# One transformer block with product-key experts on one core: split blocks inside the attention heads, scatter in pieces, four late value buffers, two row dots per ranked head

## The reference, cut to what matters

```python
mod = silu(c) @ w_ada + b_ada                         # six rows of 1024
h = rmsnorm(x) * (1 + scale1) + shift1
qa, ka, va, qb, kb, vb, ga, gb = split(h @ w_in)      # 512,128,128,512,512,512,1024,1024
ya = swa_sink_attention(rope(qa), rope(ka), va) @ w_up_swa    # 8 heads, 2 kv heads, window 128
yb = stick_breaking_attention(qb, kb, vb) @ w_up_sb           # 8 heads, causal
x = x + gate1 * ((sigmoid(ga) * ya + sigmoid(gb) * yb) @ w_out)
h2 = rmsnorm(x) * (1 + scale2) + shift2
# PEER: per head two lists of 128 key scores, the best 16 of each, the best 16 of their sums
# -> 8 x 16 experts of 128 x 128 for each token, softmax gate g
act = gelu(h2 . expert_u[e]) * g[e];   x = x + gate2 * sum_e act[e] * expert_v[e]
out = rmsnorm(x)
```

## Time and profile before

| | us |
|---|---|
| median of 3 runs (1956.57 to 1959.97) | 1956.68 |
| the profiled execution, device time | 1958.36 |
| its span, first to last instruction | 1956.4 |
| TensorE busy | 1815.1 |
| VectorE busy | 1325.8 |
| ScalarE busy | 693.5 |
| GpSimd busy | 535.2 |
| mean granted clock of TensorE | 0.949 |

### The profile page before, as it was taken

One profiled execution on the slowest core, in us unless ns is written; L12 is line 12 of the kernel. 1 busy time (PEld: TensorE's weight loads), 2 busy tenths in 40 slices (PEclk: granted clock), 3 DMA queues, 4 the chain that ended last, 5 costly groups with the idle time before them and its releaser, 6 DMA issues.

```text
span 1956.4 us, 24506 instructions
## 1 busy us (share of the span) xinstructions
PE 1815.1 (93%) x8747; PEld 1500.4 (77%) x8747; DVE 1325.8 (68%) x2755; ACT 693.5 (35%) x1072; POOL 535.2 (27%) x326
## 2 busy tenths in 40 slices
PE   5899999989988999989989969999999999999996
PEld 4555555558867999979989959999999987777774
DVE  5423232335437699989788848888877888888886
ACT  2231415153326444334343323333333333333333
POOL 0000000000004576460000035545553443333330
PEclk7989798889998999989999989999999999999998
DMA  8414030202222434346888799999998989999992
GB/s 314 179 43 150 12 139 21 86 7 90 93 90 81 143 119 144 98 160 164 221 241 226 204 324 377 338 344 335 339 339 297 324 311 341 342 338 341 344 342 107
DMA packets 221696, 416.21 MB, mean 213 GB/s; under 512 B 112305, under 2 KB 148145, under 8 KB 217649
## 3 DMA queue, kind: packets, MB, share of 16 engines
q1 hardware_dynamic: 173232, 257.70, 39.3%
q0 software_dynamic: 37440, 142.62, 20.5%
q10 hardware_dynamic: 10944, 14.95, 2.2%
HBM read 373.01 MB, written 42.21 MB: 212 GB/s over the span
## 4 chain that ended last, share of the span: by engine, by line
PE 74%; DVE 10%; DMA 5%; ACT 5%; issue 4%; SPq 2%; POOL 0%; DVEq 0%; ACTq 0%
PE bank L729 22%; PE bank L785 19%; PE bank L691 6%; PE bank L584 4%; PE bank L709 4%; DMA u_raw<-euT 4%; PE bank L625 3%; PE bank L773 2%; PE bank L619 2%; PE bank L588 1%; ACT v_split L1051 1%; DVE hot_j L1361 1%; PE bank L613 1%; DVE weights L1395 1%; DVE row_sum L1350 1%
## 5 line engine op out<-in xcount | busy, mean ns | idle before, releaser
L729 PE MATMUL bank<-h_split,u_split 128*128 128x384 f32 x3072 | 564.3, 340 | 18.3 <-DVE u_split L1339 15.7
L785 PE MATMUL bank<-v_split,a_split 128*128 128x512 f32 x2304 | 547.4, 393 | 21.8 <-DVE a_split L1400 20.0
L729 PEld LDWEIGHTS bank<-h_split,u_split 128*128 128x128 f32 x3072 | 541.0, 190 | 24.7 <-DVE u_split L1339 16.0
L785 PEld LDWEIGHTS bank<-v_split,a_split 128*128 128x128 f32 x2304 | 428.3, 188 | 127.6 <-issue 40.7
L506 POOL DMA_INDIRECT rows<-eu,idx x128 | 184.7, 1443 | 401.6 <-DVE dots L1243 376.7
L506 POOL DMA_INDIRECT rows<-ev,idx x128 | 180.4, 1410 | 269.7 <-DVE row_sum L1350 238.4
L1051 ACT ACTIVATE v_split<-v_raw 128x1024 fp32r<-128x1024 f32 x128 | 135.6, 1059 | 178.9 <-PE bank L785 174.9
L953 ACT ACTIVATE gelus<-bank 128x384 f32<-128x384 f32 x128 | 62.9, 491 | 352.7 <-PE bank L729 349.6
L1383 DVE TENSOR_TENSOR v_split<-v_raw,v_split 128x1024 fp32r<-128x1024 f32 x128 | 156.5, 1223 | 18.5 <-ACT v_split L1051 18.1
L1350 DVE SCALAR_TENSOR_TENSOR row_sum<-rows,agate,row_sum 128x1024 f32<-128x1024 f32 x127 | 162.6, 1280 | 4.3
L1339 DVE TENSOR_TENSOR u_split<-u_raw,u_split 128x1024 fp32r<-128x1024 f32 x90 | 109.9, 1221 | 74.3 <-ACT u_split L944 73.8
(11 more groups left out here) (207 smaller groups left out, 2058.3 us busy)
## 6 DMA issues: line engine op xcount, KB each, us to landing
u_raw<-euT SPq DMA_DIRECT2D x128, 512.0 KB
v_raw<-ev SPq DMA_DIRECT2D x128, 512.0 KB
arena<-w_ada SPq DMA_DIRECT2D x12, 2048.0 KB, 7.9
gates_scratch<-stage SPq DMA_DIRECT2D x12, 2048.0 KB, 19.6
gates<-gates_scratch SPq DMA_DIRECT2D x128, 192.0 KB
gelu_scratch<-gelus ACTq DMA_DIRECT2D x76, 192.0 KB, 2.9
gelus<-gelu_scratch SPq DMA_DIRECT2D x76, 192.0 KB
arena<-w_units SPq DMA_DIRECT2D x24, 512.0 KB, 3.5
```

Of the source, the lines that this page charges most:

```text
L729: last = pe.matmul(ps[6 + b][:, 0:TD], us[:, b, wp, k * P:(k + 1) * P], hs[:, xp, k, 0:TD], start=(k == 0 and q == 0), stop=(k == DC - 1 a ...
L785: last = pe.matmul(ps[2 * t + f][:], ar[:, b, ap, t * P:(t + 1) * P], vs[:, b, vp, f * 512:(f + 1) * 512], start=(first and q == 0), stop= ...
```

## The change

1. Projections, attention and units. `BLOCKS` is one list of 50 split blocks: a lead of six (k, va, q, qb, kb, v of pair 0), 28 that fill the eight heads (`FILL`: seven per pair; all 16 gate blocks are among them), 8 up and 8 out. h is split once, at the start. ScalarE makes the high parts (`block_high`), GpSimd all low parts (`block_low`). v is projected transposed and turned by TensorE (`turn_values`). Queries are stored padded with zeros to 128 rows, one copy per head. The four stick-breaking score tiles are packed into three banks, and these scores come before the window's. Sums and turned probabilities stand after the second filling block. The loops over pairs are written out. w_ada parts 4 to 11 come through one slot, one per head. In the up and out phase all eight remainders of the merged tile stand behind the last merge.
2. Two dots per head in ranking (`DOTS_HEAD` = 2), 14 in all, with their gathers on GpSimd.
3. `BEFORE` = 8 chunks instead of 4 between hot stage and main loop, with 2 dots each: STASHED = 80, NF = 48.
4. The scatter of a round is cut in eight transfers of 512 KB, with a u load after each of the second to seventh.
5. In the late stretch, four buffers for v and a (`v_late`, `a_late`, in memory that the scores have left), and in VectorE's stream the order weights, v remainder, a remainder, row sums. The last four chunks are multiplied tile by tile.

```diff
-STASHED = EARLY + BESIDE + 4
+BEFORE = 8
+STASHED = EARLY + BESIDE + BEFORE
+LATE = 4
+PIECES = 8
-DOTS_HEAD = 0
+DOTS_HEAD = 2
-DOTS_G = DOTS_RANK + GROUPS // 8 + 8
-DOTS_BY = 36
-ACC_FROM = 37
-ACC_F = 42
+DOTS_G = DOTS_RANK + GROUPS // 8 + 2 * BEFORE
+DOTS_BY = 30
+ACC_FROM = 31
+ACC_F = 48
+FILL = [[("gate", 0), ("gate", 1), ("v", 1), ("gate", 2)],
+        [("q", 1), ("qb", 1), ("kb", 1)],
...
+        [("gate", 9), ("gate", 10), ("gate", 11), ("gate", 12)],
+        [("gate", 13), ("gate", 14), ("gate", 15)]]
+LEAD = [("k", 0), ("v", -1), ("q", 0), ("qb", 0), ("kb", 0), ("v", 0)]
+SB_AT = ((0, 0), (1, 0), (2, 0), (1, 384))
+SB_ORDER = (0, 2, 1, 3)
...
             for n in range(GROUPS // 16):
...
-                for i0 in range(0, NK, NK // 2):
-                    sp.dma_start(gates_dram[i0:i0 + NK // 2, :, n * 64:n * 64 + 64].rearrange("i j t -> j i t"),
-                                 stages[n % 2][:, i0:i0 + NK // 2, :]).then_inc(g_out[n % 2], 16)
+                for k in range(PIECES):
+                    i0 = k * NK // PIECES
+                    sp.dma_start(gates_dram[i0:i0 + NK // PIECES, :, n * 64:n * 64 + 64].rearrange("i j t -> j i t"),
+                                 stages[n % 2][:, i0:i0 + NK // PIECES, :]).then_inc(g_out[n % 2], 16)
+                    if 1 <= k <= 6:
+                        u_load(EARLY + RING + 6 * (n + 1) + k - 1)
...
+            def block_low(t):
+                pool.wait_ge(w_hi, t + 1)
+                nc.gpsimd.tensor_tensor(ws[:, t % 2, 1, :], wraw[:, t % 4, :], ws[:, t % 2, 0, :].bitcast(F32), ALU.subtract).then_inc(w_split, 1)
...
+            def block(t, bank):
+                pe.wait_ge(w_split, t + 1)
+                before = [s for s in range(max(0, t - 4), t) if BANK[s] == bank]
+                if before:
+                    evacuated(pe, before[-1])
+                for k in range(DC):
+                    if t == 0:
+                        pe.wait_ge(h1_split, k + 1)
+                    for q, (wp, xp) in enumerate(PASSES):
+                        last = pe.matmul(ps[bank][:], ws[:, t % 2, wp, k * P:(k + 1) * P], h1s[xp][:, k, :],
+                                         start=(k == 0 and q == 0), stop=(k == DC - 1 and q == 2))
+                last.then_inc(block_done, 1)
...
+            for n in range(HEADS):
+                i, a = n // 2, n % 2
+                heads_scores(n)
+                for k, b in enumerate(FILL[n]):
+                    if k == 1 and n:
+                        pe.wait_ge(ob_out, n)
+                    if k == 2:
+                        if b[0] == "kb":
+                            pe.wait_ge(oa_out, n)
+                            rotate(i + 1)
+                        turn_probs(n)
+                        later_sums(n)
+                    block(AT[b], BANK[AT[b]])
+                head_outputs(n)
+                if a == 0 and i + 1 < PAIRS:
+                    turn_values(i + 1)
...
-            values(NK - 2, 0)
-            values(NK - 1, 1, final=True)
+            for t in range(ND):
+                for e in range(LATE):
+                    values(NK - LATE + e, a_late[:, e], v_late[:, e], tiles=[t], final=(e == LATE - 1))
...
+            def block_high(t):
+                sa.wait_ge(w_in[t % 4], 16 * (t // 4 + 1))
+                if t >= 2:
+                    sa.wait_ge(block_done, t - 1)
+                act_(ws[:, t % 2, 0, :], wraw[:, t % 4, :], ACT.Copy).then_inc(w_hi, 1)
...
+            for i in range(NF, NK):
                 if i + 1 < NK:
+                    weights(i + 1)
                     v_low(i + 1)
+                    a_low(i + 1)
+                for k in range(accs_before(i), accs_before(i + 1)):
+                    add_row(k)
```

More of the change, by code:

```diff
@@ L663, in _, with gates_before, evacuated @@
-            pe.wait_ge(oa_out, 2 * PAIRS + FREE)
-            pe.wait_ge(ob_out, 2 * PAIRS + FREE)
+            def gates_before(t):
+                return sum(kind == "gate" for kind, _ in BLOCKS[:t])
+            def evacuated(engine, t):
+                kind, m = BLOCKS[t]
+                if kind in "kq":
+                    engine.wait_ge(q_raw_ready, 1 if kind == "k" else m + 2)
+                elif kind == "qb":
+                    engine.wait_ge(qb_ready, m + 1)
+                elif kind == "kb":
+                    engine.wait_ge(kb_ready, m + 1)
+                elif kind == "v":
+                    engine.wait_ge(v_raw_ready, m + 2)
+                elif kind == "gate":
+                    engine.wait_ge(gate_kept, m + 1)
@@ new lines, in rotate, with turn_values @@
+            def rotate(i):
+                pe.wait_ge(q_raw_ready, i + 2)
+                pe.wait_ge(rope_ready, i + 1)
+                pe.matmul(ps[7][:], cst[:, K_ROT:K_ROT + P], qraw, start=True, stop=True).then_inc(rot_done, 1)
+            def turn_values(i):
+                pe.wait_ge(v_raw_ready, i + 2)
+                for t in range(TT):
+                    last = pe.transpose(ps[3][:, t * P:(t + 1) * P], vT[:, t * P:(t + 1) * P], ident)
+                last.then_inc(v_turned, 1)
@@ new lines, in _ @@
+            pe.wait_ge(masks_ready, 1)
+            pe.wait_ge(padded, 1)
+            block(0, BANK[0])
+            block(1, BANK[1])
+            pe.wait_ge(q_raw_ready, 1)
+            pe.matmul(ps[7][:], cst[:, K_ROT:K_ROT + P], qraw, start=True, stop=True).then_inc(rot_done, 1)
+            block(2, BANK[2])
+            turn_values(-1)
+            block(3, BANK[3])
+            rotate(0)
+            block(4, BANK[4])
+            block(5, BANK[5])
+            pe.wait_ge(v_ready, 1)
+            turn_values(0)
@@ L685, in _ @@
                             pe.wait_ge(m_split, k + 1)
-                    elif kind == "gate":
-                        bank, first, end = 4 * (m % 2) + c, k == 0, k == DC - 1
                     else:
@@ new lines, in _ @@
+            for k in range(DC):
+                ve.wait_ge(x_in, 16)
+                nv.tensor_tensor(h[:, k, :], x[:, k, :], rstd[:], ALU.mult).then_inc(norm_part, 1)
+            ada_product(2, 3, 0, 1)
+            ve.wait_ge(ada_direct, 1)
+            ve.sem_inc(ring_free[2], 1)
+            ve.wait_ge(ada_summed, 3)
+            step(nv.tensor_tensor(mod[:, 0:16], ps[6][:, 0:16], sml[:, S_B:S_B + 16], ALU.add))
+            nv.scalar_tensor_tensor(mul1[:], part(1), 1.0, sml[:, S_G1:S_G1 + DC], ALU.add, ALU.mult).then_inc(mod_ready, 1)
@@ L1509 @@
         "xT": tiles(np.asarray(x)[0].T), "small": small, "consts": constants(), "pos": np.asarray(positions),
-        "w_ada": ada, "w_kava": tiles(kv), "w_pair": pair, "w_gate": gate, "w_units": units, "w_qry": qry,
+        "w_ada": ada, "w_blocks": blocks, "w_qry": qry,
         "skT": skT, "euT": eu, "ev": np.asarray(expert_v)[0].reshape(NK, P, D), "eu": np.asarray(expert_u)[0],
```

753 lines of the change are left out of this document (398 added, 355 removed).

## The result

The changed kernel takes 1801.01 us (median of 4 runs, 1797.41 to 1802.43) where the kernel before takes 1958.33 (1956.57 to 1960.12): a ratio of 0.9194, 95% interval 0.9176 to 0.9212. The forecast was 1829 with a range of 1808 to 1862. The direction was right and the gain was larger than the range allowed: 157 us instead of 128.

The account below looks back on a forecast made before the run. TensorE, busy 93% of the span, was taken to bound the kernel. Terms -87 + 2 - 10 - 3 - 22 - 8 = -128 us from 1956.4, plus 2.0 less 1.7, gave 1829 us; range 1808 to 1862.

Parts of the forecast that it names:

- A: Projections, attention and units: split blocks filling the heads end this part at 495 us instead of 582, -87; bounds -103, -47.
- Eight heads: 138: Attention: TensorE's work in eight heads besides their blocks, from 15.6 us a head plus 1.7 added, 138 us.
- 12 for waits and clock: Attention: 12 us allowed for waits and lower clock in the eight heads.
- clock stays low: Rival for attention: the granted clock does not rise with padding, +40, total 1869 us; chance 0.12.
- B: Ranking: two row dots per head on VectorE make the last head leave later, +2 us; bounds 0 and 18.
- C: Hot stage: scatter in eight pieces with u loads between removes TensorE's waits for stage copies, -10 us; bounds -12, +3.
- D: Before the value loop: eight chunks instead of four, stretch 59.5 us by DMA bytes, net -3 us; bounds -18, +6.
- E: Late stretch: four value buffers and new order remove most of 27 us over pace, -22 us; bounds -27, +7.
- the DMA rival: Late stretch: DMA at 319 GB/s makes a chunk 4.6 us, +29, total 1858 us; chance 0.12.
- F: Tail: last four chunks tile by tile leave 8.7 us after TensorE instead of 17.0, -8 us; bounds -9, -5.
- The rivals on GpSimd's subtraction and VectorE in ranking: Block subtractions from 6.5 us each give 1957 us and more, chance 0.03; ranking's dots fall into no gap, +16, 1845, chance 0.05.
- Better than forecast: Case with the stretch before the value loop at TensorE's pace and attention without waits, 1802 us; chance 0.06.

Follow-up runs that it names:

- experiment 1: Also called rows64: changed kernel with both score stages' products over the head's 64 rows instead of 128 padded ones; 1824.06 us, +23.1.
- experiment 3: Changed kernel with only the four stick-breaking score products of a head over 64 rows, window products still padded; 1802.53 us.
- experiment 4: Changed kernel with the 34 projection and gate blocks as 8 plain float32 products each instead of 24 split ones; 1847.58 us, +46.6.
- experiment 2: Kernel before the change with queries padded to 128 rows in its old attention, all else as it was; 1923.01 us against 1956.26, ratio 0.9836.
- Experiment 6: Changed kernel without the 14 row dots in ranking, their rows taken up in the value loop and late stretch; 1791.51 us, -9.5.
- experiment 5: Changed kernel with the scatter in two pieces instead of eight and each group's six u loads ahead of it; 1822.72 us, +21.7.
- experiment 7: Changed kernel with four score chunks instead of eight between the hot stage and the value loop; 1800.36 us, no difference.
- experiment 8: Changed kernel without ranking dots, fewer row dots before the value loop: eight chunks with one each 1782.75 us, with none 1773.88; four with none 1783.86.
- rows0_8: Changed kernel without ranking dots and without row dots in the eight chunks before the value loop; 1773.88 us, 0.9068 of the time before.
- experiment 9: Changed kernel's late stretch with two value buffers, new order, last two chunks tile by tile: 1807.68 us; with four buffers, old order: 1807.30 us.

## Why the prediction was too careful

**A, -87 forecast, -108.4 measured, beyond its bound of -103.** By its own terms: the first block starts at 55.7 instead of 50 (TensorE waits for VectorE's low part of the activations, 8.6 us), +5.7; the lead is 1.5 us over its blocks and the 5 that I gave it; units and their start (369.2 to 474.0) 104.8 against 105. The heads came to 274.4 instead of 302: this is the step that failed. "Eight heads: 138" was 122.1 (274.4 less 28 blocks of 5.44), 15.3 a head where I had 17.3, and the "12 for waits and clock" were nothing. I took the head's own work from the one head at full clock in the old trace and did not see that its 64-row window products were themselves slow there: experiment 1 prices that at 1.5 us a head, 12 us in all, and experiment 3 adds 0.3 a head for the stick-breaking scores. It was to be read in the trace that I had, in the rows from 136.45 on under experiment 3: pairs 0.94 us apart at the full clock. About 0.2 us a head of the difference stays unexplained. What makes up the 108 is, by the runs: 48 the split blocks (experiment 4), 27 the padding (experiment 1), the rest, some 33, filling in place of waits and the moved units, if these parts add up.

**The clock.** The step "the change pads the queries, so I expect most of the low stretches to go" was right, and experiment 2 shows it in the old kernel too. The cause that I had in mind, 64-row products as such, was too wide: experiment 3 has 64-row products in a row at full clock. Rows64 brings the low level back with the window products, which alternate with 128-row ones; that it is the alternation is argued and not shown, since three heads of rows64 and one of the kernel before have it at full clock. The rule of the Trainium skill that idle gaps bring the lower level (TensorE: Matmul & The Clock Gate, Why this matters for your kernels) agrees in direction with what is left, a clock of 0.96 where a pair has 6 us of gaps and of 0.87 in the stretch with 21 us of waits, and does not account for the heads of rows64, which have no gap. The rival "clock stays low" is out.

**B, +2 forecast, +7.1.** Inside its bounds. VectorE did find room for the 14 dots, as I said; GpSimd's queue did not. Each gather stood ahead of a remainder that TensorE waits for, and I had named that queue without a price for it. Experiment 6 shows it: the 7.1 us come back, 4.2 of them at these remainders and 1.9 at the handover.

**C, -10 forecast, -19.4, beyond its bound of -12.** The mechanism was right. The bound was the one wait row that I took for the whole; there were VectorE's waits beside it (2.2 in experiment 5), and the clock behind them (3.4). The stage's own window in the earlier trace rows had 14.4 us between length and busy time; that was a better bound, and with the low clock inside the busy time it comes to 17.8 of the 19.4.

**D, -3 forecast, +3.2; by experiment 7 the edit alone is worth nothing.** The sum of bytes by the best rate was the right tool and gave 63 of the 65.7 us; the 3.5 that I took off it, because loads no longer queue behind all of the scatter, were not there. What I missed is that more than half of those bytes were a choice: 4.2 of the 7.1 MB are rows that nothing needs there (experiment 8).

**E, -22 forecast, -32.5, beyond its bound of -27.** The stall went as forecast and further, to zero. The bound was too small because the pace was: I gave a value chunk half of a pair by its columns, 4.17 us. It takes 4.10 (336.5 us for 82 chunks, 1.7 of them for other products) and the score chunk 4.19 (1448.80 to 1452.99 on the timeline), since products carry a part that doesn't depend on columns: 18 x 227 ns against 24 x 175. With 4.10 the old stretch had 32 us over pace, not 27. The 5 that I kept back were not needed, and the DMA rival did not come at 338 GB/s here, nor at 354 in rows0_8.

**F, -8 forecast, -8.2.** Right, and experiment 9 gives its slope: two chunks instead of four tile by tile leave 5.6 us.

**The rivals on GpSimd's subtraction and VectorE in ranking** are out: 2.43 us each, and VectorE is busy 251 of 286 us. A, C and E gave 41 us more than forecast, each beyond the bound written beside it, and B and D cost 11 more; that is the 30 us by which the sum was off. "Better than forecast" had been put down to D and to A without waits; A without waits was true and D was not, so that its 1802 meets the measured 1801 by luck.

## What to carry to other kernels

Take the price of a group of products from its spacing and compare it with neighbours of another shape: a short list of half-height products between full-height ones can cost time of its own and, behind it, the clock of a busy engine; here padding them, or keeping them in a run of their own, avoided both. Where a stage is bound by the DMA queues, list what each moved piece brings with it in bytes, and move only what is needed there; work that fills a wait gains nothing if it carries as many bytes as the queues move in its time. Bound a gain by the difference between a window's length and its busy time, and by the low clock inside the busy time, not by the one wait row that names your mechanism.

## What the runs showed of the hardware that I had not expected

Window products of 64 rows alternating with mask products of 128 rows are 0.94 us apart per pair where those with 128 rows are 0.55 apart, and behind five of eight such heads the granted clock falls (to 0.64 over the 5 us behind the first) with TensorE busy throughout; four stick-breaking products of 64 rows in a row cost 0.27 us a head and leave the clock at 1.00. A split product of 512 columns takes 227 ns and one of 384 takes 175, which at 2.4 GHz leaves 13 to 15 ns that don't depend on the columns. DMA queues at a share of 0.94 to 0.95 (351 to 354 GB/s) for 720 us, loop and late stretch of rows0_8, left TensorE without a wait.
